# First tile of the next stage taken from pre-scaled copies of x and y, the residual update of that tile done later, five constant matmuls for six

## The chip, the cores and the metric

One Trainium2 chip, one core. The time is that of one launch in device microseconds: the median of three runs for the kernel before, beside the span of one profiled execution. Smaller is better.

## What is computed

Two layers of an encoder step over 320 tokens (256 of a new stream, 64 of a running one), width 1024. The residual x passes three sub-layers per layer, and each is wrapped in two norms:

```python
h = _rms_norm(x, P['ffn1_norm_pre'][l])
x = x + 0.5 * _rms_norm(_swiglu(h, P['ffn1_w_up'][l], P['ffn1_w_down'][l]), P['ffn1_norm_post'][l])
h = _rms_norm(x, P['mix_norm_pre'][l])
m, k_rows, v_rows, s_gla, s_ret = _mixer(h, l, P, past_k, past_v, s_gla0, s_ret0)
x = x + _rms_norm(m, P['mix_norm_post'][l])
h = _rms_norm(x, P['ffn2_norm_pre'][l])
x = x + 0.5 * _rms_norm(_swiglu(h, P['ffn2_w_up'][l], P['ffn2_w_down'][l]), P['ffn2_norm_post'][l])
# _rms_norm(x, g) = x * rsqrt(mean(x * x) + EPS) * g
```

The mixer projects h by W_in, runs a gated linear recurrence, differential attention and retention, and projects by W_out.

## The kernel before, in words

Everything lies transposed: x and y are 8 tiles of 128 features by 320 tokens. Each product is made of three fp32r matmuls (`product`, L629): a weight tile is split into a rounded part w_h (ACT, `hi`) and the rest w_l (DVE, `lo`), and an activation tile into xn_h (ACT, `split_hi`, L1020) and xn_l (DVE, `split_lo`, L1299). Weights come by DMA into six slots.

There are six sub-layers in a row, so five **boundaries** at which a sub-layer's result y is added to x and the next sub-layer starts: in the order of the run, feed-forward 1 to mixer, mixer to feed-forward 2, layer 0 to layer 1, and the first two again in layer 1. At a boundary:

- PE sums the squares of y over the features (`stat_y`, L676 and L680), ACT takes the root (L1025), DVE the reciprocal (L1306), and PE spreads it over the partitions into PSUM, `ps_rs` (`spread`, L688). Then PE runs `keep_busy(6)`: six matmuls of constants whose result nobody reads (L695, two passes each in the trace, so 12 records).
- DVE (`post`) multiplies the y tiles, which already hold the gain of the norm behind the sub-layer, by `ps_rs` (`add_first`, L1310, semaphore y_norm). It adds tile 0 to x itself (L1317); POOL adds tiles 1 to 7 (`add_y`, L519), each when its y tile is multiplied. The semaphore of both is x_new.
- ACT (`pre`) makes xn_h of tile k as soon as x_new says so, and squares x tile k - 1 into y (L1030, semaphore sq_x). DVE makes xn_l of the tile.
- PE's `opening` takes the four first output tiles feature tile by feature tile: step k needs xn_l of tile k and is 12 matmuls. Since the norm in front of the sub-layer is applied to the output, its sum of squares is wanted late: DVE adds squares 0 to 3 (`sum_x`, L1333 to L1337), POOL squares 4 to 7 (L527), and PE takes both in behind step 6 (`stat_x`, L664 and L668). Behind step 7 it spreads the reciprocal (L688 again), for which DVE has first to get through `sum_x`, two `lo` (L511), at the first boundary a few small instructions on the attention's lambda, and L1306.

Every engine works through its own instructions in order; semaphores join them. What stands in `post` and `pre` is therefore the order on DVE and ACT.

Of the kernel before, what the change touches and what calls it, by code (L numbers as in the profile page):

```python
# [9 lines left out]
ACT = mybir.ActivationFunctionType  # L10
ALU = mybir.AluOpType
# [5 lines left out]
T = T_P + T_S  # L17
KD = D // P
KF = D_FF // P
# [22 lines left out]
G_OUT = G_MIX + N_MIX  # L42
G_F2 = G_OUT + N_OUT
GROUPS = G_F2 + KF + KD
# [208 lines left out]
def build(nc, ins, outs, table_at):  # L253
    ctx = ExitStack()
    with ctx:
# [3 lines left out]
        def sem(name):  # L259
            return ctx.enter_context(nc.semaphore(name))  # L260
# [7 lines left out]
        x = sb("x", [P, KD, T])  # L268
        y = sb("y", [P, KD, T])
# [114 lines left out]
        raw_in = [sem(f"raw_in{s}") for s in range(SLOTS)]  # L384
        w_hi, w_lo, w_used = sem("w_hi"), sem("w_lo"), sem("w_used")
        evac = sem("evac")
        x_new = sem("x_new")
        y_norm = sem("y_norm")
        xn_hi, xn_lo = sem("xn_hi"), sem("xn_lo")
        sq_x = sem("sq_x")  # L390
# [113 lines left out]
        def lo(dve, l, u, i=0):  # L504

            if u >= UNITS:
                l, u = l + 1, u - UNITS
            if l < DEPTH:
                s, cols = slot(l, u), blocks_of(u) * P
                dve.wait_ge(w_hi, 6 * i + (l * UNITS + u + 1))  # L510
                dve.tensor_tensor(w_l[s][:, 0:cols], raw[s][:, 0:cols], w_h[s][:, 0:cols], ALU.subtract).then_inc(w_lo, 1)  # L511

        @block.gpsimd
        def _(pool):
            def add_y(l, m):

                for k in range(1, KD):
                    pool.wait_ge(y_norm, (l * 3 + m) * KD + k + 1)
                    pool.tensor_tensor(x[:, k, :], x[:, k, :], y[:, k, :], ALU.add).then_inc(x_new, 1)  # L519

            def sum_x(l, n):
# [104 lines left out]
        def _(pe):  # L626
# [65 lines left out]
            def keep_busy(n):  # L692

                for _ in range(n):
                    pe.matmul(ps_stat[:, 128:384], C("ident"), const[:, 0:256], start=True, stop=True, skip_group_check=True)  # L695

            def ffn(l, u0, g0, norm, n, m):

                def up_pair(i, q, free):
                    pe.wait_ge(w_lo, 6 * i + (l * UNITS + u0 + 2 * q + 2))  # L700
                    if free:
                        pe.wait_ge(evac, 3 * i + (l * GROUPS + g0 + q - 2))
                    for g in range(2):
                        tile_part(slot(l, u0 + 2 * q + g), 2 * q + g, 0, KD)

                opening(l, u0, n, norm, m)
                up_pair(0, 2, False)
                with pe.Fori(1, KF // 3) as i:
                    for q in range(3):
                        up_pair(i, q, True)  # L710
                up_pair(KF // 3, 0, True)
                def down_pair(i):
                    for b in range(2):
                        pe.wait_ge(evac, 2 * i + (l * GROUPS + g0 + KF + b - 1))
                        for t, (a, z_) in enumerate(THIRD):
                            u = u0 + N_UP + 3 * b + t
                            pe.wait_ge(w_lo, 6 * i + (l * UNITS + u + 1))
                            pe.wait_ge(hid_lo, (l * 2 + norm // 4) * KF + z_)
                            for k in range(a, z_):
                                mm = product(ps[:, 2 + b, 0:T], slot(l, u), k - a, hid_h[:, k, :], hid_l[:, k, :], k == 0, k == KF - 1)  # L720
                            mm.then_inc(w_used, 1)
                with pe.Fori(0, KD // 2 - 1) as i:
                    down_pair(i)
                last = l == DEPTH - 1 and norm == 4
                if last:
                    pe.wait_ge(evac, l * GROUPS + g0 + KF)
                    turned(x, X_BANK, 0, KD, x_turn)
                down_pair(KD // 2 - 1)
                stat_y(l, norm + 1, norm // 2)
                if last:  # L730
                    pe.wait_ge(evac, l * GROUPS + g0 + KF + KD - 1)
                    pe.wait_ge(x_turned, 6)
                    turned(y, Y_BANK, 0, KD - 1, y_turn)
                    pe.wait_ge(evac, l * GROUPS + g0 + KF + KD)
                    turned(y, Y_BANK, KD - 1, KD, y_turn)
                else:
                    spread(l, norm + 1)
                    keep_busy(6)

            def turned(t, banks, k0, k1, done):  # L740

# [224 lines left out]
            for l in range(DEPTH):  # L966
                ffn(l, U_F1, G_F1, 0, 0, 0)
                opening(l, U_MIX, 1, 2, 1)
                pe.wait_ge(tables_loaded, PIECES * 16)
                pe.wait_ge(pick_loaded, 16)  # L970
                for kind, *arg in SCHEDULE:
                    if kind == "part":
                        v, k0, k1 = arg
                        if k0 == 0:
                            pe.wait_ge(w_lo, l * UNITS + U_MIX + v + 1)
                            if G_PRIOR[v] is not None:
                                pe.wait_ge(evac, l * GROUPS + G_MIX + G_PRIOR[v] + 1)
                        tile_part(slot(l, U_MIX + v), G_BANK[v], k0, k1)
                    else:
                        mixer_step(l, kind, arg[0] if arg else None)  # L980
                for v in range(OPENING, N_OUT):
                    pe.wait_ge(w_lo, l * UNITS + U_OUT + v + 1)
                    if v >= 6:
                        pe.wait_ge(evac, l * GROUPS + G_OUT + v - 5)
                    tile_part(slot(l, U_OUT + v), v % 6, 0, KD, HEAD_ORDER, xw_h, xw_l)
                stat_y(l, 3, 1)
                spread(l, 3)
                keep_busy(6)
                ffn(l, U_F2, G_F2, 4, 3, 2)


# [3 lines left out]
        def _(act):  # L995
# [20 lines left out]
            def split_hi(l, n, k, src, gain):  # L1016

                scale = 1.0 if gain is None else gains[l][:, gain, k:k + 1]
                dst = xw_h if gain is None else xn_h
                act.activation(dst[:, k, :], src[:, k, :], ACT.Copy, scale=scale).then_inc(xn_hi, 1)  # L1020
# [6 lines left out]
            def pre(l, n, norm, m, u0):  # L1027

                def square(k):
                    act.activation(y[:, k, :], x[:, k, :], ACT.Square).then_inc(sq_x, 1)  # L1030

                for k in range(KD):
                    act.wait_ge(x_new, (l * 3 + m) * KD + k + 1)
                    split_hi(l, n, k, x, norm)
                    if l == 0 and n == 0 and k < 2:
                        hi(act, l, u0 + k + 2)
                    if k:
                        square(k - 1)
                square(KD - 1)
                for v in (4, 5):  # L1040
                    hi(act, l, u0 + v)
                act.preload_act_table(ACT.Sqrt)
                root(l, norm)
# [204 lines left out]
        def _(dve):  # L1248
# [54 lines left out]
            def root(l, n):  # L1303

                dve.wait_ge(ss_sqrt, l * 6 + n + 1)
                dve.reciprocal(inv[:, 0:3], var[:, 0:3]).then_inc(inv_out, 1)  # L1306
                dve.wait_ge(rs_mm, l * 6 + n + 1)

            def add_first(k):
                dve.tensor_tensor(y[:, k, :], y[:, k, :], ps_rs[:, 0:T], ALU.mult).then_inc(y_norm, 1)  # L1310

            def post(l, n, norm, update):

                if update:
                    add_first(0)
                    dve.drain()
                    dve.tensor_tensor(x[:, 0, :], x[:, 0, :], y[:, 0, :], ALU.add).then_inc(x_new, 1)  # L1317
                    add_first(1)
                    add_first(2)
                for k in range(KD):  # L1320
                    if norm is not None:
                        split_lo(l, n, k, x, norm, k)
                    if l == 0 and n == 0 and k == 0:
                        dve.wait_ge(w_lo, 2)
                        lo(dve, l, 2)
                        lo(dve, l, 3)
                    if update and k + 3 < KD:
                        add_first(k + 3)

            def sum_x(l, m):  # L1330

# [30 lines left out]
            def ffn(l, u0, g0, norm):  # L1362
# [50 lines left out]
                if l == DEPTH - 1 and f == 1:  # L1413
                    rows_out(l, norm + 1)
                else:
                    root(l, norm + 1)
                    dve.wait_ge(evac, l * GROUPS + g0 + KF + KD)

# [167 lines left out]
            for l in range(DEPTH):  # L1586
# [34 lines left out]
                for v in range(N_OUT):  # L1621
                    if v < KD - 1:
                        add_square(l, v, 1, v % 2)
                    if v < 5:
                        lo(dve, l, U_OUT + 6 + v)
                    if v == N_OUT - 2:
                        lo(dve, l, U_F2 + 3)
                root(l, 3)
                dve.wait_ge(evac, l * GROUPS + G_OUT + N_OUT)
                begin(l, 3, 4, 2, U_F2, True)  # L1630
# [38 lines left out]
```

## Time and profile before

| | us |
|---|---|
| median of 3 runs | 1392.91 |
| range of these | 1391.44 to 1393.98 |
| profiled execution, its own time | 1392.57 |
| its span, first to last instruction | 1390.8 |
| PE busy / DVE / ACT / POOL | 1352.7 / 804.0 / 634.2 / 132.1 |
| mean granted TensorE clock | 0.989 of 2.4 GHz |

Engines: PE is TensorE's matmul, PEld its weight load, DVE VectorE, ACT ScalarE, POOL GpSimd. A line such as `258.03 0.49 DVE L1317 ...` is the start in us from the span's start, the length, engine, source line, operation and tiles; in brackets stands how long the engine had been idle and what ended that. One engine's entries can overlap by some 0.08 us, since it starts the next instruction while the last one runs out. A line that ends in x2 or more is several instructions taken together.

### The profile page before, as it was taken

What the parts mean: (1) busy time and instruction counts of PE and PEld (TensorE: products, weight loads), DVE (VectorE), ACT (ScalarE), POOL (GpSimd) and SP (SyncE); (2) the same over time, 40 slices, a digit from 0 to 9 for tenths busy, and PEclk for the clock granted to TensorE, in tenths of its full rate; (3) what the DMA queues carried; (4) which work ended last, traced back from release to release, by engine and by line L of the source; (5) the groups of instructions that cost most, each with busy time, mean ns of one, the idle gap of its engine ahead of it and who ended that gap; (6) DMA issues with size and microseconds to landing.
All of it is one profiled execution on the core that took longest, in us unless ns stands there. A gap on an engine that the chain in (4) does not pass through costs nothing.

```text
span 1390.8 us, 24882 instructions
## 1 busy us (share of the span) xinstructions
PE 1352.7 (97%) x9709; PEld 1312.9 (94%) x9709; DVE 804.0 (58%) x1230; ACT 634.2 (46%) x1001; POOL 132.1 (9%) x131
## 2 busy tenths in 40 slices
PE   6999999999989999999999999999899999999998
PEld 6999999988879999999999999999789799999998
DVE  4655543676665665554366555447876477555542
ACT  4544443553455544443355444445435555444333
POOL 2000000361000200000020000003700011000000
PEclk9999999999999999999999999999999899999999
DMA  5655555453234455545545554455333245555552
GB/s 150 191 168 168 164 164 148 127 142 86 80 115 107 107 150 150 151 144 151 152 113 151 148 147 144 144 158 147 87 91 90 89 122 137 151 150 147 144 147 70
DMA packets 351754, 187.51 MB, mean 135 GB/s; under 512 B 6320, under 2 KB 348604, under 8 KB 351688
## 3 DMA queue, kind: packets, MB, share of 16 engines
q1 hardware_dynamic: 348368, 177.49, 45.3%
q0 software_dynamic: 2480, 8.10, 1.7%
q10 hardware_dynamic: 840, 0.99, 0.2%
q8 instruction: 46, 0.75, 0.2%
q14 instruction: 20, 0.16, 0.0%
HBM read 182.24 MB, written 4.33 MB: 134 GB/s over the span
## 4 chain that ended last, share of the span: by engine, by line
PE 90%; DVE 3%; ACT 2%; DMA 2%; issue 1%; DVEq 1%; ACTq 0%; POOL 0%; SPq 0%; POOLq 0%
PE ps L632 28%; PE ps L634 27%; PE ps L633 27%; DMA raw<-in_w_in_dram 1%; PE ps L830 1%; PE ps L931 1%; PE ps L688 1%; PE ps L695 1%; DVE w_l L511 1%; PE ps L805 1%; PE ps L903 1%; ACT w_h L502 1%; PE ps L941 0%; DMA par_in<-in_ret_norm_dram 0%; PE ps L909 0%
## 5 line engine op out<-in xcount | busy, mean ns | idle before, releaser
L632 PE MATMUL ps<-xn_l,w_h 128*128 128x320 f32 x1840 | 579.8, 315 | 2.7 <-DVE xn_l L1299 2.3
L633 PE MATMUL ps<-xn_h,w_l 128*128 128x320 f32 x1840 | 568.9, 309 | 0.0
L634 PE MATMUL ps<-xn_h,w_h 128*128 128x320 f32 x1840 | 568.8, 309 | 0.0
L511 DVE TENSOR_TENSOR w_l<-raw,w_h 128x1024 fp32r<-128x1024 f32 (+1 forms) x340 | 409.0, 1205 | 180.2 <-ACT w_h L502 180.1
L502 ACT ACTIVATE w_h<-raw 128x1024 fp32r<-128x1024 f32 (+1 forms) x342 | 353.4, 1036 | 250.7 <-DMA raw<-in_ffn_w_down_dram 131.8
L632 PEld LDWEIGHTS ps<-xn_l,w_h 128*128 128x128 f32 x1840 | 346.5, 188 | 12.3 <-issue 4.1
L633 PEld LDWEIGHTS ps<-xn_h,w_l 128*128 128x128 f32 x1840 | 346.8, 188 | 0.7
L634 PEld LDWEIGHTS ps<-xn_h,w_h 128*128 128x128 f32 x1840 | 346.5, 188 | 0.0
L632 PE MATMUL ps<-hid_l,w_h 128*128 128x320 f32 x704 | 217.0, 308 | 0.0
L633 PE MATMUL ps<-hid_h,w_l 128*128 128x320 f32 x704 | 216.9, 308 | 0.0
L634 PE MATMUL ps<-hid_h,w_h 128*128 128x320 f32 x704 | 216.9, 308 | 0.0
L632 PEld LDWEIGHTS ps<-hid_l,w_h 128*128 128x128 f32 x704 | 131.9, 187 | 0.0
L633 PEld LDWEIGHTS ps<-hid_h,w_l 128*128 128x128 f32 x704 | 131.9, 187 | 0.0
L634 PEld LDWEIGHTS ps<-hid_h,w_h 128*128 128x128 f32 x704 | 131.9, 187 | 0.0
L1368 DVE TENSOR_TENSOR gate<-ps,rs 128x320 f32<-128x320 f32 x72 | 35.3, 491 | 152.2 <-PE ps L634 152.0
L1065 ACT ACTIVATE gate<-gate 128x320 f32<-128x320 f32 x72 | 34.0, 472 | 138.5 <-DVE gate L1368 138.5
L519 POOL TENSOR_TENSOR x<-x,y 128x320 f32<-128x320 f32 x35 | 37.0, 1088 | 352.7 <-DVE y L1310 352.7
L1069 ACT ACTIVATE hid_h<-up 128x320 f32 (+1 forms) x72 | 34.0, 473 | 67.8 <-DVE up L1374 67.8
L1374 DVE TENSOR_TENSOR up<-up,gate 128x320 f32<-128x320 f32 x72 | 35.4, 492 | 12.0 <-issue 10.9
L1166 ACT ACTIVATE probs<-probs,tiny 128x128 f32<-128x128 f32 (+2 forms) x40 | 19.2, 482 | 49.2 <-DVE tiny L1498 49.2
L1050 ACT ACTIVATE sq<-ps 128x320 f32<-128x320 f32 x48 | 20.8, 432 | 45.9 <-PE ps L634 45.8
L632 PE MATMUL ps<-xw_l,w_h 128*128 128x320 f32 x128 | 41.4, 324 | 0.0
(242 smaller groups left out, 1159.7 us busy)
## 6 DMA issues: line engine op xcount, KB each, us to landing
raw<-in_ffn_w_up_dram SPq DMA_DIRECT2D x176, 512.0 KB, 3.8
raw<-in_ffn_w_down_dram SPq DMA_DIRECT2D x64, 448.0 KB, 3.8
raw<-in_w_in_dram SPq DMA_DIRECT2D x54, 512.0 KB, 3.8
raw<-in_ffn_w_down_dram SPq DMA_DIRECT2D x32, 512.0 KB, 4.1
raw<-in_w_out_dram SPq DMA_DIRECT2D x16, 512.0 KB, 4.1
const<-in_tables_dram POOLq DMA_DIRECT2D x8, 298.0 KB, 4.5
x_in<-in_x_prompt_dram SPq DMA_DIRECT2D x1, 1024.0 KB, 6.6
scores<-in_cache_diff_k_dram POOLq DMA_DIRECT2D x2, 512.0 KB, 5.3
```

Source lines behind the costliest of these rows:

```text
L502: act.activation(w_h[s][:, 0:cols], raw[s][:, 0:cols], ACT.Copy).then_inc(w_hi, 1)
L511: dve.tensor_tensor(w_l[s][:, 0:cols], raw[s][:, 0:cols], w_h[s][:, 0:cols], ALU.subtract).then_inc(w_lo, 1)
L519: pool.tensor_tensor(x[:, k, :], x[:, k, :], y[:, k, :], ALU.add).then_inc(x_new, 1)
L632: pe.matmul(out, w_h[s][:, w], xl, start=first, stop=False)
L633: pe.matmul(out, w_l[s][:, w], xh, start=False, stop=False)
L634: return pe.matmul(out, w_h[s][:, w], xh, start=False, stop=last)
L1050: act.activation(sq[b][:, :], ps[:, bank, 0:T], ACT.Square).then_inc(y_sq, 1)
L1065: act.activation(gate[q][:, :], gate[q][:, :], ACT.Silu).then_inc(silu, 1)
L1069: act.activation(tile(hid_h, v), up[q][:, :], ACT.Copy).then_inc(hid_hi, 1)
L1166: i = act.activation(p, p, ACT.Exp, bias=tiny[:, 8 + 2 * s + m:9 + 2 * s + m], accum_out=tiny[:, 12 + 2 * s + m:13 + 2 * s + m])
L1368: dve.tensor_tensor(gate[q][:, :], ps[:, 2 * q, 0:T], rs[:, :], ALU.mult).then_inc(up_mul, 1)
L1374: dve.tensor_tensor(up[q][:, :], up[q][:, :], gate[q][:, :], ALU.mult).then_inc(prod, 1)
```

## The change

Five places. While PE still sums y's squares, DVE (`prepare_first`) writes two products with the gain of the next norm: x tile 0 into sq[0] and y tile 0 into ssum_x. When `ps_rs` is there, `first_tile` multiplies ssum_x by it and adds it to sq[0]; ACT copies this (no scale any more) into xn_h tile 0, and DVE takes xn_l tile 0 from it. x tile 0 itself is updated behind xn_l tile 2, so ACT squares tiles 0 to 2 only behind xn_h tile 3. `add_first(k + 3)` behind xn_l tile k becomes `add_first(k + 2)`, and POOL's counts on y_norm follow the new order 1, 2, 3, 0, 4 ... 7. `keep_busy` runs five matmuls.

```diff
@@ gpsimd, add_y
                 for k in range(1, KD):
-                    pool.wait_ge(y_norm, (l * 3 + m) * KD + k + 1)
+                    pool.wait_ge(y_norm, (l * 3 + m) * KD + (k if k < 3 else k + 1))
                     pool.tensor_tensor(x[:, k, :], x[:, k, :], y[:, k, :], ALU.add).then_inc(x_new, 1)
@@ tensor, ffn and behind the mixer
-                    keep_busy(6)
+                    keep_busy(5)
@@ scalar, pre
+                update = l * 3 + m
                 for k in range(KD):
-                    act.wait_ge(x_new, (l * 3 + m) * KD + k + 1)
-                    split_hi(l, n, k, x, norm)
+                    if update and k == 0:
+                        act.wait_ge(x_scaled, update)
+                        act.activation(xn_h[:, 0, :], sq[0][:, :], ACT.Copy).then_inc(xn_hi, 1)
+                    else:
+                        act.wait_ge(x_new, KD + (update - 1) * (KD - 1) + k if update else k + 1)
+                        split_hi(l, n, k, x, norm)
...
-                    if k:
+                    if update and k == 3:
+                        act.wait_ge(x_first, update)
+                        square(0)
+                        square(1)
+                        square(2)
+                    elif k and (not update or k > 3):
                         square(k - 1)
@@ vector
+            def prepare_first(l, norm, evicted):
+
+                gain = gains[l][:, norm, 0:1]
+                dve.wait_ge(evac, evicted)
+                dve.drain()
+                dve.tensor_scalar(sq[0][:, :], x[:, 0, :], gain, None, ALU.mult)
+                dve.tensor_scalar(ssum_x[:, :], y[:, 0, :], gain, None, ALU.mult)
+                dve.drain()
+
+            def first_tile(l, n, update):
+
+                dve.tensor_tensor(ssum_x[:, :], ssum_x[:, :], ps_rs[:, 0:T], ALU.mult)
+                dve.drain()
+                dve.tensor_tensor(sq[0][:, :], sq[0][:, :], ssum_x[:, :], ALU.add).then_inc(x_scaled, 1)
+                add_first(1)
+                dve.wait_ge(xn_hi, l * 32 + 8 * n + 1)
+                dve.tensor_tensor(xn_l[:, 0, :], sq[0][:, :], xn_h[:, 0, :], ALU.subtract).then_inc(xn_lo, 1)
+                add_first(2)
+
             def post(l, n, norm, update):
 
                 if update:
-                    add_first(0)
-                    dve.drain()
-                    dve.tensor_tensor(x[:, 0, :], x[:, 0, :], y[:, 0, :], ALU.add).then_inc(x_new, 1)
-                    add_first(1)
-                    add_first(2)
+                    first_tile(l, n, update)
                 for k in range(KD):
-                    if norm is not None:
+                    if k or not update:
                         split_lo(l, n, k, x, norm, k)
...
-                    if update and k + 3 < KD:
-                        add_first(k + 3)
+                    if update and k == 2:
+                        add_first(0)
+                        dve.drain()
+                        dve.tensor_tensor(x[:, 0, :], x[:, 0, :], y[:, 0, :], ALU.add).then_inc(x_first, 1)
+                    if update and 1 <= k + 2 < KD and k:
+                        add_first(k + 2)
@@ vector, before root(l, norm + 1) at the end of ffn, and before root(l, 3)
+                    prepare_first(*((l, 2) if f == 0 else (l + 1, 0)), l * GROUPS + g0 + KF + 1)
...
+                prepare_first(l, 4, l * GROUPS + G_OUT + 1)
```

## Rows read from the trace of the kernel before

**Rows 1.** The page: the span, and the shares of the chain that ended last.

```profile
span 1390.8 us, 24882 instructions
PE 90%; DVE 3%; ACT 2%; DMA 2%; issue 1%; DVEq 1%; ACTq 0%; POOL 0%; SPq 0%; POOLq 0%
```

**Rows 2.** Timeline of DVE at the first boundary (start, us, instruction, idle before).

```profile
256.25 0.18 DVE L1306 RECIPROCAL inv<-var 128x3 f32<-128x3 f32 x1 [1.68 <-ACT var L1025]
257.45 0.49 DVE L1310 TENSOR_TENSOR y<-y,ps 128x320 f32<-128x320 f32 x1 [1.03 <-PE ps L688]
258.03 0.49 DVE L1317 TENSOR_TENSOR x<-x,y 128x320 f32<-128x320 f32 x1
258.44 0.88 DVE L1310 TENSOR_TENSOR y<-y,ps 128x320 f32<-128x320 f32 x2
259.23 0.97 DVE L1299 SCALAR_TENSOR_TENSOR xn_l<-x,par,xn_h 128x320 fp32r<-128x320 f32 x1
...
260.53 0.77 DVE L1299 SCALAR_TENSOR_TENSOR xn_l<-x,par,xn_h 128x320 fp32r<-128x320 f32 x1
...
267.04 0.81 DVE L1299 SCALAR_TENSOR_TENSOR xn_l<-x,par,xn_h 128x320 fp32r<-128x320 f32 x1 [0.28 <-ACT xn_h L1020]
267.77 1.17 DVE L1333 SCALAR_TENSOR_TENSOR ssum<-y 128x320 f32<-128x320 f32 x1
...
270.10 0.49 DVE L1337 TENSOR_TENSOR ssum<-ssum,y 128x320 f32<-128x320 f32 x1
270.51 2.35 DVE L511 TENSOR_TENSOR w_l<-raw,w_h 128x1024 fp32r<-128x1024 f32 x2
...
274.32 0.18 DVE L1306 RECIPROCAL inv<-var 128x3 f32<-128x3 f32 x1
```

**Rows 3.** Timeline of ACT at the same boundary.

```profile
258.56 0.56 ACT L1020 ACTIVATE xn_h<-x,par 128x320 fp32r<-128x320 f32 x1 [0.82 <-DVE x L1317]
259.90 0.56 ACT L1020 ACTIVATE xn_h<-x,par 128x320 fp32r<-128x320 f32 x1 [0.78 <-POOL x L519]
260.36 0.46 ACT L1030 ACTIVATE y<-x 128x320 f32<-128x320 f32 x1
```

**Rows 4.** Timeline of POOL there: its first addition alone, all seven, the last two sums.

```profile
259.00 0.86 POOL L519 TENSOR_TENSOR x<-x,y 128x320 f32<-128x320 f32 x1 [1.06 <-DVE y L1310]
259.00 7.40 POOL L519 TENSOR_TENSOR x<-x,y 128x320 f32<-128x320 f32 x7 [1.06 <-DVE y L1310]
...
267.64 2.04 POOL L527 TENSOR_TENSOR ssum_x<-ssum_x,y 128x320 f32<-128x320 f32 x2
```

**Rows 5.** Timeline of PE there: constants, first product, sum of x's squares, spread.

```profile
257.25 2.76 PE L695 MATMUL ps<-const 128*128 128x256 f32 x12
260.26 0.41 PE L632 MATMUL ps<-xn_l,w_h 128*128 128x320 f32 x1 [0.26 <-DVE xn_l L1299]
...
272.68 0.72 PE L664 MATMUL ps<-const,ssum 128*128 128x1 f32 x6
...
275.78 0.83 PE L688 MATMUL ps<-const,inv 128*128 128x128 f32 x6
```

**Rows 6.** The group of ACT's copies without a scale (min/median/max ns).

```profile
L1020 ACT ACTIVATE xw_h<-y x16: 470/473/476, 415.5 to 1117.6; 128x320 fp32r<-128x320 f32 x16
```

**Rows 7.** Timeline of PE at the second and the third boundary.

```profile
457.93 3.79 PE L695 MATMUL ps<-const 128*128 128x256 f32 x12
461.37 0.50 PE L632 MATMUL ps<-xn_l,w_h 128*128 128x320 f32 x1
...
698.85 4.44 PE L695 MATMUL ps<-const 128*128 128x256 f32 x12
702.94 0.50 PE L632 MATMUL ps<-xn_l,w_h 128*128 128x320 f32 x1
```

**Rows 8.** Busy time by stretch: window, length, PE, PEld, DVE, ACT, POOL, granted clock, DMA.

```profile
457.00:458.00 1.00, 1.00 (x7) 1.00 (x6) 0.00 (x0) 0.00 (x0) 0.00 (x0) 0.50 0.21 63
...
700.00:701.00 1.00, 1.00 (x4) 0.80 (x3) 1.00 (x4) 0.56 (x1) 0.41 (x1) 0.50 0.00 0
940.00:943.00 3.00, 3.00 (x17) 2.38 (x15) 2.42 (x5) 0.63 (x2) 1.92 (x4) 1.00 1.01 340
```

**Rows 9.** Timeline of DVE at the second boundary: the reciprocal, and the tiles' start.

```profile
456.30 0.17 DVE L1306 RECIPROCAL inv<-var 128x3 f32<-128x3 f32 x1 [1.48 <-ACT var L1025]
458.17 0.49 DVE L1310 TENSOR_TENSOR y<-y,ps 128x320 f32<-128x320 f32 x1 [1.70 <-PE ps L688]
...
459.96 0.97 DVE L1299 SCALAR_TENSOR_TENSOR xn_l<-x,par,xn_h 128x320 fp32r<-128x320 f32 x1
```

More of the change, by code:

```diff
@@ L386, in build @@
         evac = sem("evac")
-        x_new = sem("x_new")
+        x_new, x_first = sem("x_new"), sem("x_first_tile")
+        x_scaled = sem("first_tile_times_next_gain")
         y_norm = sem("y_norm")
@@ L987, in _ @@
                 spread(l, 3)
-                keep_busy(6)
+                keep_busy(5)
                 ffn(l, U_F2, G_F2, 4, 3, 2)
```

## The prediction

> **What bounds the kernel now.** I read the page first: PE carries 90% of the chain that ended last [rows 1], so an edit on DVE, ACT or POOL counts only where PE waits for it. It can do that at the five boundaries, so I went through the timelines of all engines there. At the first one, take DVE's first multiply behind the spread, 257.45, as zero; all times below count from it. The multiply runs to 0.49, the update of x tile 0 from 0.58 to 1.07, two more multiplies to 1.87, and xn_l of tile 0 from 1.78 to 2.75 [rows 2]. ACT's part lies between, 1.11 to 1.67 [rows 3]. The constants end at 2.56, the first product starts at 2.81, released by xn_l [rows 5]. So this chain binds by 0.25 us. Then PE doesn't wait: seven steps bring it to the sum of x's squares at 15.23, and its spread stands at 18.33 [rows 5]. DVE has its sum of squares ready at 13.14 (270.10 + 0.49) and POOL at 12.23 [rows 2, 4]: 2.1 us to spare.
>
> The two boundaries around the mixer in layer 1, the fourth and fifth, repeat this within 0.03 us. The second and third differ: the granted clock is 0.50 there, the lower level of 1.2 GHz, while it is 1.00 at the fourth [rows 8]. The constants then take 3.79 and 4.44 us instead of 2.76 [rows 5, 7], and it is they that end last: at the second, xn_l is ready at 460.93 [rows 9], the first product starts at 461.37 [rows 7].
>
> **A collision that sets the prices.** POOL's first addition takes 0.86 us; seven take 7.40, so 1.09 each once DVE works beside it [rows 4]. DVE's xn_l of tile 0 takes 0.97 beside that first addition, which ends at 2.41, 0.34 before xn_l does; L1333 takes 1.17 beside POOL's sums, L1337 only 0.49 after them [rows 2, 4]. Every DVE instruction with both inputs in SBUF behaves so, and the multiplies by PSUM do not (0.49 and 0.44 each). I read it as taking turns: whoever comes second waits for the other to finish. DVE then needs 0.34 more (0.49 alone), POOL 0.75 (0.86 alone). With handovers of 0.04 us from DVE to ACT (258.52 to 258.56) and from POOL to ACT (259.86 to 259.90), and 0.08 from DVE to POOL (the first of the two multiplies ends at 258.92, POOL starts at 259.00) [rows 2 to 4], stepping through the old order with these prices gives 13.12 for DVE's sums and 12.20 for POOL's, against 13.14 and 12.23 in the trace. I use the same prices for the new order.
>
> The Trainium skill's page "SBUF — State Buffer", section "Who interferes with whom", says the same as a rule: a DVE instruction with two SBUF inputs and a GpSimd one that reads SBUF exclude each other, and order of issue decides who waits. By that rule the change's first tile can't be early, since its subtraction has two SBUF inputs; the trace agrees with the rule (0.97 against 0.49).
>
> **prepare_first.** Two instructions of at most 0.49 us and two drains of about 0.09, some 1.1 us. DVE sat idle for 1.68 us before this reciprocal at the first boundary and 1.48 at the second [rows 2, 9]; the other three lie at about 1.6. Hidden, cost 0. If the cover went, each 0.1 us would be 0.1 us of PE's wait for the spread. No row shows a DVE instruction of this kind beside the four DMAs that POOL issues there; from both sides, 0 to +0.3 us at two boundaries; I take 0, because the preparation is nearly through when they start.
>
> **The first tile.** Multiply to 0.49, addition to 1.07, as before. ACT's copy has no scale and takes 0.47 for 0.56 [rows 3, 6]: 1.11 to 1.58. One multiply less stands ahead of xn_l, so DVE is ready at 1.62 instead of 1.87. But POOL starts on tile 1 at 1.55 as before and holds its turn to 2.41. So xn_l ends at 2.75 as before, and the first product starts at 2.81 as before. Gain 0; if DVE came first, it would end at 2.11, a gain of up to 0.65. The margin is 0.07 us; I take 0, by the row of 0.97.
>
> **Five constants.** Two passes less, 2.76 / 12 x 2 = 0.46 us. At three boundaries xn_l binds, and PE only idles 0.7 us instead of 0.25: gain 0. At the second the constants would end at 460.91, xn_l at 460.93: gain 0.38. At the third they still bind: gain about 0.44.
>
> **The later tiles.** This is where I see the cost. y tile 2 is multiplied behind xn_l tile 0 (2.66 to 3.13, before: 1.39 to 1.87), so POOL, which used to have work waiting, starts tile 2 at 3.21 and xn_l tile 1, at 3.06, now goes ahead of it: tile 2 on POOL ends at 4.30 for 3.48. xn_h of tile 2 follows to 4.90, xn_l to 5.43. POOL's tile 3 waits for a count of 4 on y_norm, which is the multiply of tile 0, placed behind xn_l tile 2: it ends at 5.83. POOL adds tile 3 from 5.91 to 6.77 (before: 3.46 to 4.57), and the late update of x tile 0 waits for its turn to 7.11. xn_h of tile 3 to 7.37, xn_l to 7.92. Queued behind on ACT are three squares, 7.28 to 8.48, so xn_h of tile 4 starts at 8.71. From there each y multiply is one tile less ahead than before, and the rest goes at DVE-to-POOL-to-ACT round-trip pace: xn_l ends at 9.77, 10.65, 12.49, 13.58 for tiles 4 to 7.
>
> Does PE wait in its steps? Step k starts at 3.05 + 1.76 k (15.37 less 3.05 over seven steps): 8.33 for tile 3 (ready 7.92), 10.09 for tile 4 (9.77), 13.61 for tile 6 (12.49). No, by 0.3 us at the closest. But tile 7 is ready at 13.58 instead of 10.40 (267.04 + 0.81 [rows 2]), and DVE's three sums come behind it: 2.8 us as before, so 16.34. PE wants them at 15.37, the start of its first of six (the row's 15.23 holds 0.14 of overlap), and starts at 16.39: a new wait of 1.0 us. POOL's sums, at 15.4, are not last.
>
> **Behind that.** DVE's two `lo` move to 18.6 (15.41 + 3.2), the reciprocal to 18.8; PE wants its spread at 18.47 + 1.0 = 19.5, so this is covered at four boundaries. At the first, small instructions stand between, and the reciprocal starts at 16.87, 1.46 behind the `lo` [rows 2]: it ends at 20.2, PE starts at 20.3 instead of 19.5: +0.8 us more, once.
>
> **The sum.** First boundary 1.0 + 0.8; fourth and fifth 1.0 each. At the second PE starts its steps at 3.20 and wants the sums 0.5 later than at the first: the floor of 16.39 costs 0.5 in all. At the third it starts at 3.89, the floor lies 0.2 below the old time: -0.2. Together 1.8 + 0.5 - 0.2 + 2.0 = **+4.1 us**. The profiled execution took 1392.57 us (span 1390.8), 0.34 below the median of the runs, so its boundaries stand for the median's; 1392.9 + 4.1 = **1397.0 us**.
>
> **Bounds.** If the turns fall better (POOL and DVE never meet at tiles 3 and 5), the sums come 0.7 us sooner: +0.3 per boundary, 0.5 for the first's spread, minus 0.8 for the constants, so about +1. If two more turns go against DVE, 0.45 each, the sums come 0.9 later: +4.5 in all, 1401.5.
>
> **Rivals.**
> (a) *Hidden.* The sums come by 15.4 after all, and only the constants count: -0.8 us, 1392.1. For it: 2.1 us of slack before. Against it: tile 0's detour alone puts POOL's tile 3 back by 2.4 us against the seven close additions before [rows 4]. 15%.
> (b) *As the edit is built.* DVE's subtraction goes ahead of POOL's tile 1, PE starts 0.65 sooner at three boundaries, and the sums are in time: 3 x 0.65 + 0.8 = 2.8, so 1390.1 us. It decides at 0.07 us of order, and needs (a) too. 6%. (That the first tile is not earlier, the change not doing what it says, is part of my forecast.)
> (c) *The clock.* With the pause of PE before the first step grown from 0.25 to 0.7 us and 1 us of waiting at the sums, the lower level comes at more boundaries. It costs 5.1 - 4.0 = 1.1 us at one (reciprocal to first product, 461.37 - 456.30 against 260.26 - 256.25 [rows 2, 5, 7, 9]), and three boundaries are still free of it: 1397.0 + 3.3 = 1400.3. It bites from the second extra boundary on. For it: the pauses are longer. Against it: the pause before the constants (2.6 us), which the clock fell behind, is unchanged. 13%.
> The forecast keeps 66%.
>
> **Numbers.** A measurement of this kernel tells about 0.2% (2.8 us) from no change: above 1395.7 is slower, below 1390.1 faster. The forecast spreads from 1394 to 1399.5 and is slower in nine of ten cases, 0.59; with (c), 0.72. Same: the rest of the forecast and (a), 0.22. Faster: 0.06. The range 1392.8 to 1401.3 takes in the bounds and part of (a).
>
> **What would show it.** In the changed kernel's profile: PE idle before L664 (about 1 us at three boundaries, released by DVE's ssum, L1337's place), which has none now; the first product still 2.8 us behind DVE's first multiply, and the subtraction at 0.7 us or more; a gap in POOL's additions between tiles 2 and 3 of about 1.6 us; a wait before the spread at the first boundary only; the reciprocal of y at its old distance from ACT's root. I am wrong if L664 shows no wait, if POOL's additions run on closely, or if the subtraction of tile 0 takes 0.49.

## The result and the profile after

The changed kernel takes 1404.05 us (median of 6 runs, 1402.72 to 1407.83); the kernel before, in the same session, 1392.19 (1391.21 to 1393.98). The ratio is 1.0086, interval 1.0075 to 1.0096: **11.9 us slower**. The forecast was 1397.0, in a range that ended at 1401.3. The sign and the place were right; the forecast loss of 4.1 us was a third of what came.

The page of the changed kernel, its span and the shares of the chain that ended last (lines of [rows 1]):

```profile
span 1401.9 us, 24897 instructions
...
PE 86%; DVE 6%; ACT 3%; DMA 2%; POOL 1%; DVEq 1%; issue 1%; SPq 0%; ACTq 0%; POOLq 0%
```

PE fell from 90% to 86% of the chain, DVE rose from 3% to 6%, and ACT and POOL have a part. The waits of PE say where (engine and line, for whom, us in total, times, longest):

```profile
PE ps L665 <- DVE ssum L1367: 4.4, 5, 1.1
PE ps L689 <- DVE inv L1317: 4.2, 6, 1.3
```

The first line is new. Before, PE never waited for the sum of x's squares; now it does at all five boundaries. L1367 is the old L1337, L665 the old L664.

The timeline of DVE at the fourth boundary of the changed kernel, which answers to [rows 2] (the first multiply behind the spread is at 944.88):

```profile
944.88 0.49 DVE L1334 TENSOR_TENSOR ssum_x<-ssum_x,ps 128x320 f32<-128x320 f32 x1 [1.03 <-PE ps L689]
945.45 0.49 DVE L1336 TENSOR_TENSOR sq<-sq,ssum_x 128x320 f32<-128x320 f32 x1
945.86 0.48 DVE L1321 TENSOR_TENSOR y<-y,ps 128x320 f32<-128x320 f32 x1
946.48 1.16 DVE L1339 TENSOR_TENSOR xn_l<-sq,xn_h 128x320 fp32r<-128x320 f32 x1
...
950.90 1.21 DVE L1356 TENSOR_TENSOR x<-x,y 128x320 f32<-128x320 f32 x1
...
957.97 0.80 DVE L1310 SCALAR_TENSOR_TENSOR xn_l<-x,par,xn_h 128x320 fp32r<-128x320 f32 x1 [0.29 <-ACT xn_h L1021]
958.69 1.17 DVE L1363 SCALAR_TENSOR_TENSOR ssum<-y 128x320 f32<-128x320 f32 x1
...
961.03 0.49 DVE L1367 TENSOR_TENSOR ssum<-ssum,y 128x320 f32<-128x320 f32 x1
```

And POOL there, which answers to [rows 4]:

```profile
946.43 0.85 POOL L520 TENSOR_TENSOR x<-x,y 128x320 f32<-128x320 f32 x1 [0.98 <-DVE y L1321]
948.11 1.12 POOL L520 TENSOR_TENSOR x<-x,y 128x320 f32<-128x320 f32 x1 [0.83 <-DVE y L1321]
950.89 0.88 POOL L520 TENSOR_TENSOR x<-x,y 128x320 f32<-128x320 f32 x1 [1.66 <-DVE y L1321]
952.59 1.96 POOL L520 TENSOR_TENSOR x<-x,y 128x320 f32<-128x320 f32 x2 [0.82 <-DVE y L1321]
```

The subtraction for xn_l of tile 0 (946.48) starts 0.05 us after POOL's first addition (946.43), takes 1.16 us and ends at 947.64, 2.76 behind the first multiply, where the kernel before had 2.75. The shorter first tile brought nothing. POOL, which made its seven additions without a pause, now stops 0.83, 1.66 and 0.82 us for y. The longest stop is ahead of tile 3. "The change" gives the order of the multiplies as 1, 2, 3, 0, so the one of tile 3 is the third; but the condition `k < 3` in the diff lets POOL wait for a count of 4, that is for the multiply of tile 0 as well. DVE's sums end at 961.52, 16.64 behind the first multiply, for 13.14 before.

What PE makes of this (timeline of PE, same boundary; [rows 5] before):

```profile
947.68 0.41 PE L633 MATMUL ps<-xn_l,w_h 128*128 128x320 f32 x1 [0.68 <-DVE xn_l L1339]
...
961.58 0.83 PE L665 MATMUL ps<-const,ssum 128*128 128x1 f32 x6 [1.08 <-DVE ssum L1367]
...
965.53 0.47 PE L633 MATMUL ps<-xn_l,w_h 128*128 128x320 f32 x1
...
966.33 0.83 PE L689 MATMUL ps<-const,inv 128*128 128x128 f32 x6
```

13.90 us pass from the first product to the sums, for 12.43. Then 4.75 to the spread, for 3.10: a matmul of step 7 takes 0.47 us in its row instead of 0.31. The busy times of that stretch (columns as in [rows 8]) give the granted clock as 0.50, the lower level of 1.2 GHz:

```profile
963.00:966.00 3.00, 3.00 (x12) 3.00 (x13) 0.88 (x2) 0.17 (x1) 0.00 (x0) 0.50 0.17 26
```

Before it fell, PE had stood still for 1.08 us and then run the twelve one-column records of the sums. The five boundaries side by side, in us, read from the starts of L1306, of the first product, of L664 and of L688 in the profile of each kernel:

| boundary | 1 | 2 | 3 | 4 | 5 | sum |
|---|---|---|---|---|---|---|
| reciprocal to first product, before | 4.01 | 5.07 | 5.10 | 4.02 | 4.02 | 22.2 |
| after | 4.66 | 4.70 | 4.37 | 4.00 | 4.00 | 21.7 |
| first product to sums, before | 12.42 | 12.51 | 12.51 | 12.43 | 12.43 | 62.3 |
| after | 13.25 | 13.91 | 13.51 | 13.90 | 13.90 | 68.5 |
| sums to spread, before | 3.10 | 3.10 | 3.10 | 3.10 | 3.09 | 15.5 |
| after | 3.55 | 4.27 | 3.21 | 4.75 | 4.43 | 20.2 |

So of 11.1 us of span, 6.2 lie between the first product and the sums, 4.7 behind the sums, and -0.5 ahead of the first product. The rest, 0.7, lies elsewhere. (The medians differ by 11.9 us, 0.8 more than these two profiled spans.) Of the 4.7 us, 0.45 at the first boundary are a wait for the reciprocal (0.18 us of idle time for DVE's inv stand in PE's row there); the other 4.3 go with the lower level of the clock.

The granted clock by stretch shows where that level stood. Before, it was 0.50 at the constants of the second and third boundary and 1.00 at those of the others. In the changed kernel it is 0.50 at the constants of the first, second and third, and 0.50 behind the sums at the second, fourth and fifth. The pauses of PE at the sums were 0.58, 1.09, 0.55, 1.08 and 1.08 us.

### The profile page after: what moved, and what is told of

Its sections match the earlier page's. It is cut to its first block, busy times and chain, and to the rows that moved or that the text cites. A ratio compares the mean times of both kernels' runs of the same rounds, so it can differ in the third digit from the quotient of the medians.

```text
span 1401.9 us, 24897 instructions
## 1 busy us (share of the span) xinstructions
PE 1359.8 (97%) x9699; PEld 1318.2 (94%) x9699; DVE 810.4 (58%) x1250; ACT 632.9 (45%) x1001; POOL 127.6 (9%) x131
## 4 chain that ended last, share of the span: by engine, by line
PE 86%; DVE 6%; ACT 3%; DMA 2%; POOL 1%; DVEq 1%; issue 1%; SPq 0%; ACTq 0%; POOLq 0%
PE ps L633 26%; PE ps L634 26%; PE ps L635 26%; POOL x L520 1%; DMA raw<-in_ffn_w_up_dram 1%; ACT xn_h L1021 1%; DVE xn_l L1310 1%; PE ps L689 1%; PE ps L831 1%; PE ps L932 1%; PE ps L806 1%; DMA raw<-in_w_in_dram 1%; DVE w_l L512 1%; PE ps L942 0%; PE ps L904 0%
## 5 line engine op out<-in xcount | busy, mean ns | idle before, releaser
L520 POOL TENSOR_TENSOR x<-x,y 128x320 f32<-128x320 f32 x35 | 33.9, 978 | 372.3 <-DVE y L1321 372.3
L1404 DVE TENSOR_TENSOR up<-up,gate 128x320 f32<-128x320 f32 x72 | 35.4, 492 | 11.2 <-issue 10.1
```

What stands on the lines that cost most here:

```text
L1404: dve.tensor_tensor(up[q][:, :], up[q][:, :], gate[q][:, :], ALU.mult).then_inc(prod, 1)
```

## The experiments

Theory S: the sum of x's squares comes too late because DVE and POOL get through the tiles later; PE waits, and the granted clock falls behind the wait. Rivals: C, the clock fell because a constant matmul is missing; P, the preparation or the new first tile costs the time; L, the shorter lead of the y multiplies alone.

**POOL's addition of tile 3 released by the right count (after_count3).**

```diff
-                    pool.wait_ge(y_norm, (l * 3 + m) * KD + (k if k < 3 else k + 1))
+                    pool.wait_ge(y_norm, (l * 3 + m) * KD + (k if k < 4 else k + 1))
```

> The changed kernel, with POOL's addition of tile 3 waiting for a count of 3 on y_norm (the multiply of tile 3) and not 4 (that of tile 0, behind xn_l tile 2). Theory S (the sum of x's squares comes late, PE waits for it, and the granted clock falls behind that wait): stepping through the order with the trace's prices, DVE's sums end at 15.9 behind its first multiply for 16.6, so PE's wait before L665 shrinks from 1.1 to about 0.4 us, the start of the sums moves 0.7 us forward at each of five boundaries, and some of the falls of the clock behind it go: 1404.0 - 3.5 - 2 = 1398 us. Theory C (the missing sixth constant matmul lets the clock fall): no change, 1404. Theory P (the preparation or the new first tile costs it): no change, 1404.

1399.3 us, ratio to before 1.0047 (1.0030 to 1.0064). The first product to the sums is 13.16 to 13.19 everywhere, for 13.25 to 13.91. PE's row at the fourth boundary:

```profile
959.34 0.83 PE L665 MATMUL ps<-const,ssum 128*128 128x1 f32 x6 [0.58 <-DVE ssum L1367]
```

One digit takes some 40% of the loss away, as S has it, though the wait is 0.6 us and not 0.4. The sums to the spread still take 3.5 to 4.2, and the granted clock is 0.50 behind the sums at all five boundaries of this profile, where the changed kernel had three. So the forecast that some falls would go did not come true, and a pause of 0.6 us was enough here; at the first and third boundary of the changed kernel, where the clock had been low at the constants, pauses as long brought none.

**Six constants again (after_six).**

```diff
-                    keep_busy(5)
+                    keep_busy(6)
```

> The changed kernel with six constant matmuls again. Theory S: PE waits for the sums, not for the start, so nothing moves at the boundaries where xn_l tile 0 binds, and the sums end when they did: 1404 within 1.5 us. Theory C: the falls of the clock that the change added go, 5 of them at 1 to 1.7 us each: 1397 us, with the mean granted clock back at 0.989.

1403.7 us, 1.0078 (1.0061 to 1.0095). No time came back, and the mean granted clock was 0.982 to 0.985 as in the changed kernel. C falls as the cause of the loss. But "nothing moves" was not right either: in this profile the clock was 0.50 at the constants of the first, second and fourth boundary, the first products came 2.9 us later in all than in the changed kernel, and the stretch from there to the sums was 2.5 us shorter in all. The sums set the time, whenever PE starts.

**The lead of three tiles restored, with POOL's counts to match, everything else of the change kept (after_lead3).**

```diff
-                    pool.wait_ge(y_norm, (l * 3 + m) * KD + (k if k < 3 else k + 1))
+                    pool.wait_ge(y_norm, (l * 3 + m) * KD + (k if k < 5 else k + 1))
...
                 add_first(1)
+                add_first(2)
                 dve.wait_ge(xn_hi, l * 32 + 8 * n + 1)
                 dve.tensor_tensor(xn_l[:, 0, :], sq[0][:, :], xn_h[:, 0, :], ALU.subtract).then_inc(xn_lo, 1)
-                add_first(2)
+                add_first(3)
...
-                    if update and 1 <= k + 2 < KD and k:
-                        add_first(k + 2)
+                    if update and k and k + 3 < KD:
+                        add_first(k + 3)
```

> The changed kernel, with DVE's multiplies of y again three tiles ahead (2 before xn_l tile 0, 3 behind it and so on) and POOL's counts to match. Pre-scaled first tile, late update of x tile 0, late squares, the preparation and five constants all stay. Theory S: stepping through with the trace's prices, DVE's sums end at 14.6 behind its first multiply, 0.7 us before PE wants them: no wait, clock as in the kernel before, and 0.4 us less at boundaries where the constants end last: 1392 to 1393.5 us. Theory P (preparation and first tile cost it): 1402 to 1404.

1392.4 us, 0.9996 (0.9987 to 1.0006). The whole loss is gone, with the preparation, the pre-scaled tile, the late update, the late squares and five constants still in. P falls. The new counts also take away POOL's needless wait for tile 0, so this run undoes two things together, the shorter lead and that count; after_count3 undid the count alone. DVE and PE at the fourth boundary (two timelines of this kernel):

```profile
953.91 0.49 DVE L1368 TENSOR_TENSOR ssum<-ssum,y 128x320 f32<-128x320 f32 x1
```

```profile
955.05 0.72 PE L665 MATMUL ps<-const,ssum 128*128 128x1 f32 x6
...
958.15 0.83 PE L689 MATMUL ps<-const,inv 128*128 128x128 f32 x6
```

The sums are ready 0.65 us before PE starts on them, no wait stands in PE's row, and the spread follows 3.10 later.

**Only the shorter lead, in the kernel before (before_lead2).**

```diff
                     add_first(1)
-                    add_first(2)
...
-                    if update and k + 3 < KD:
-                        add_first(k + 3)
+                    if update and k + 2 < KD:
+                        add_first(k + 2)
```

> The kernel before, with only DVE's multiplies of y one tile less ahead (tile 2 behind xn_l tile 0, tile k + 2 behind tile k). Stepping through gives DVE's sums at 14.9 for 13.1: inside the 2.1 us of slack, so no wait of PE and 1393 us within 1.5. If the shorter lead alone is the cause (rival L: it starves POOL, and the first tile's detour is innocent), PE waits at L664 and the time is 1399 us or more.

1392.5 us, 0.9997 (0.9988 to 1.0007). L falls too. The last sum ends 0.26 us before PE wants it (956.94 + 0.49 against 957.69). Behind the first multiply DVE's sums end at 13.1 in the kernel before, at 15.0 with the shorter lead alone and at 14.6 with the detour for tile 0 alone (after_lead3). Either fits into the 2.1 us of slack. Together they reach 15.9 (POOL's count put right) and 16.6 (the changed kernel), and PE wants them at 15.2.

**The late sum alone, in the kernel before**, with six copies (before_late_sum) and with eight (before_late_sum8):

```diff
                 post(l, n, norm, update)
+                if update:
+                    for _ in range(6):
+                        dve.tensor_copy(rs[:, :], ps_rs[:, 0:T])
+                        dve.drain()
                 sum_x(l, m)
```

> The kernel before, with six copies of the spread into rs (overwritten later) and a drain behind each, 6 x 0.58 = 3.5 us, ahead of DVE's sum of squares at the five boundaries. Nothing else of the change is in it: first tile, order, six constants as before. Theory S: the sums end at 16.6 behind the first multiply for 13.1, as in the changed kernel, PE waits 1.1 us at the sums and the clock falls behind it: 1392.2 + 11 = 1403 us (and at least 1392.2 + 5 x 1.4 = 1399 if the clock doesn't follow). Theories C and P: the late sum costs only its wait, 0 to 3 us, 1392 to 1395, since they put the 12 us elsewhere.

1393.1 us, 0.9997 (0.9988 to 1.0007). This missed: the copies delayed the end of the sums, counted from the first multiply, only by 2.2 to 2.5 us, since the sums no longer ran beside POOL and took 0.49 us each. At the fourth boundary they ended at 957.23 and PE started at 957.29 with no wait. As a dose it is useful: late by nearly all of the slack costs nothing.

> As before_late_sum, with eight copies for six. Six moved the end of DVE's sums only from 14.3 to 16.5 to 17.3 us behind the reciprocal (the copies also took away collisions with POOL), just under the point from which PE waits; the changed kernel has 17.8. Two more copies, 1.16 us, bring it to 17.7 to 18.0. Theory S: now PE waits 0.9 to 1.2 us at L664 at each boundary, the start of the sums moves by 1.2 to 1.5 us, and with what the clock does behind it the kernel takes 1393 + 7 to 11 = 1400 to 1404 us. If the 12 us have another source (the first tile, the order): 1393 to 1396.

1403.1 us, 1.0068 (1.0045 to 1.0091). Two copies more, and ten microseconds come. DVE and PE at the fourth boundary:

```profile
958.29 4.43 DVE L1350 COPY rs<-ps 128x320 f32<-128x320 f32 x8
962.80 0.49 DVE L1333 SCALAR_TENSOR_TENSOR ssum<-y 128x320 f32<-128x320 f32 x1
```

```profile
964.49 0.83 PE L664 MATMUL ps<-const,ssum 128*128 128x1 f32 x6 [1.10 <-DVE ssum L1337]
```

PE's waits for the sums add up to 4.6 us (4.4 in the changed kernel), the first product to the sums to 67.8 (68.5), the sums to the spread to 20.6 (20.2), and the mean granted clock of the runs lies between 0.982 and 0.988. The copies hold up everything that DVE does behind them, but PE's rows show waits for the sums at all five boundaries and for the reciprocal only at the first, 0.17 us. So a late sum by itself makes a loss of the changed kernel's size (1.0068 and 1.0086, intervals that overlap); this is shown, not argued.

**Constants in the place of the wait.** Both in the changed kernel (after_fill) and in the kernel before (before_fill):

```diff
                     if i == KD - 2:
+                        if l or n:
+                            keep_busy(3)
                         stat_x(l, norm, m)
```

> The changed kernel, with three constant matmuls (2 passes each, 1.4 us) put into PE's queue ahead of the sum of x's squares at the five boundaries, so that PE works while it would wait. If the clock falls because of PE's wait (second half of theory S), it no longer falls behind the sums, which is worth 1.2 to 1.6 us at three boundaries, while the constants are hidden in 1.1 us of wait and cost up to 0.3 us each: 1404.0 - 4 + 1 = 1401 us, with the spread starting 3.1 to 3.5 us behind L665 everywhere (now 4.3, 4.8 and 4.4 at the second, fourth and fifth). If the wait has nothing to do with the clock: 1404 to 1405.5, with as many stretches at a granted 0.5 as before.

after_fill: 1402.75 us, 1.0076 (1.0059 to 1.0093). The row of this kernel at the fourth boundary, which answers to `963.00:966.00` above:

```profile
962.00:965.00 3.00, 3.00 (x25) 3.00 (x25) 2.08 (x3) 0.22 (x2) 0.00 (x0) 1.00 0.01 3
```

The granted clock is 1.00, as it is behind the sums at the other four. The sums to the spread went back to 3.10 to 3.17 at all five boundaries, and the mean granted clock of the runs, between 0.982 and 0.985 in the changed kernel, lies between 0.986 and 0.989 here, the level of the kernel before (between 0.986 and 0.992). So the falls behind the sums came from the pause. But 4.5 us behind the sums were bought with 1.4 ahead of them and 1.2 ahead of the first product, and the total moved by 1.3, within the intervals. What the falls cost in all is not shown by this.

> The kernel before, with three constant matmuls ahead of the sum of x's squares at the five boundaries: PE reaches the sums 1.4 us late, but busy, at full clock. It prices the delay without a pause. If a delay of 1.4 us costs 1.4 us wherever it comes from, 1393.0 + 5 x 1.4 = 1400 us and the spread 3.1 us behind the sums everywhere; what the changed kernel (1404.0) and before_late_sum8 (1403.1) take beyond this is then the clock that falls behind a pause. If it takes 1403 or more, the clock has no part in it and a delay costs more than itself.

before_fill: 1402.6 us, 1.0066 (1.0053 to 1.0078). First product to sums 13.71 to 13.81, sums to spread 3.10, no wait at the sums, clock 0.987 to 0.990. This missed too: five delays of 1.3 us cost 9.2 us (by the ratio, as in the next three runs; 10.0 by the medians). In its profile 1.2 us of the excess are one landing of W_in behind the fourth boundary (PE waits 2.13 us for gv_tok there, 0.89 before), and two stretches of low clock lie elsewhere. Of its 10.1 us more of span only 5.4 lie at the boundaries. The rest lies in the two mixer stretches, from the spread of boundary 1 to the reciprocal of boundary 2 (182.95 us for 180.52) and from 4 to 5 (184.20 for 181.25); the feed-forward stretches between boundaries agree within 0.1 us. But the first of these also takes 182.98 us in the profile of before_lead2 and 182.94 in that of before_dve1 (below), whose medians are those of the kernel before. One profile of each kernel can't tell whether the delay brings this rest. Three more runs asked how the remainder goes.

> One constant matmul (0.46 us) ahead of the sum of x's squares at five boundaries of the kernel before, for three in before_fill. If a delay costs itself: 1392.8 + 2.3 = 1395.1 us. If it costs 1.5 times itself, as three constants did (9.5 us for 6.4): 1396.2. If there is a fixed cost of some 3 us as soon as PE comes late at all: 1398.

One constant (before_fill1): 1396.4 us, 1.0027 (1.0017 to 1.0037): +3.8 (2.4 to 5.2) for 5 x 0.45.

> Six constants (2.7 us) at the same place. If a delay costs itself: 1392.8 + 5 x 2.7 = 1406.3 us. At 1.5 times: 1413. With a fixed cost of 3 us: 1409.3.

Six constants (before_fill6): 1407.2 us, 1.0107 (1.0093 to 1.0122): +14.9 (13.0 to 17.0) for 5 x 2.6 = 13.

> Nine constants for six behind the spread of y's root: the same 1.4 us as in before_fill, but ahead of the first product, which waits 0.25 us for xn_l anyway, and not ahead of the sums. Each boundary is delayed by 1.1 to 1.4 us. If the remainder belongs to the place (what waits behind the sums), 1392.8 + 6.2 = 1399 us. If any delay of PE costs 1.5 times itself, 1402.

Nine constants (before_nine): 1398.4 us, 1.0040 (1.0026 to 1.0053): +5.6 (3.6 to 7.4). The first product came 0.7 us later where the clock was full and 1.3 where it was low, which is 3 x 0.7 + 2 x 1.3 = 4.7 us with the clock as in the kernel before.

In these four runs a delay costs itself plus 1 to 3 us that don't grow in step with it. Neither "1.5 times" (it forecast 1413 for six) nor a fixed 3 us (1398 for one lies outside) is right for all; where that rest lies is **left open**.

**A better opening.** DVE adds tile 1 (before_dve1), or tiles 1 and 2 (before_dve2), to x itself, with five constants (here tile 1; for two tiles, POOL starts at 3, and the block stands for `k < 2` with `x[:, k + 1, :]` and `add_first(k + 2)`):

```diff
-                for k in range(1, KD):
+                for k in range(2, KD):
...
                     add_first(1)
-                    add_first(2)
                 for k in range(KD):
                     if norm is not None:
                         split_lo(l, n, k, x, norm, k)
+                    if update and k == 0:
+                        dve.drain()
+                        dve.tensor_tensor(x[:, 1, :], x[:, 1, :], y[:, 1, :], ALU.add).then_inc(x_new, 1)
+                        add_first(2)
...
-                    keep_busy(6)
+                    keep_busy(5)
```

> The kernel before, with DVE adding y tile 1 to x itself, between xn_l tile 0 and the multiply of tile 2, and five constants. POOL has nothing to do when xn_l tile 0 is made, so that should take 0.55 us for 0.97 and the first product start 0.45 to 0.5 us earlier at the boundaries where xn_l binds. xn_l tile 1 then meets POOL's tile 2 and ends at 4.6 behind the first multiply, 0.2 us after PE wants it. Net 0.2 to 0.4 us less at each of five boundaries: 1393.2 - 1.5 = 1391.7 us, and the sums still in time (13.9). If the taking of turns is not what delays xn_l tile 0, it starts where it did: 1393 us, xn_l at 0.97.

1393.1 us, 0.9999 (0.9990 to 1.0009). DVE at the fourth boundary:

```profile
942.60 0.55 DVE L1299 SCALAR_TENSOR_TENSOR xn_l<-x,par,xn_h 128x320 fp32r<-128x320 f32 x1 [0.23 <-ACT xn_h L1020]
943.24 0.49 DVE L1324 TENSOR_TENSOR x<-x,y 128x320 f32<-128x320 f32 x1
943.65 0.88 DVE L1310 TENSOR_TENSOR y<-y,ps 128x320 f32<-128x320 f32 x2
944.44 0.99 DVE L1299 SCALAR_TENSOR_TENSOR xn_l<-x,par,xn_h 128x320 fp32r<-128x320 f32 x1
```

With POOL idle xn_l of tile 0 takes 0.55 us, for 0.97, and the first product comes 3.50 behind the reciprocal, for 4.02. Tile 1 then meets POOL, takes 0.99, and PE gives the half microsecond back in step 1 (12.96 to the sums for 12.43).

> As before_dve1, with DVE adding y tile 2 to x as well, behind xn_l tile 1, and POOL starting with tile 3. before_dve1 moved the first product 0.5 us forward (3.50 us behind the reciprocal for 4.02) and lost it in step 1 (12.96 us from the first product to the sums for 12.43), since xn_l tile 1 met POOL's tile 2 and took 0.99 us. Now POOL is idle then: xn_l tile 1 should take 0.55, tile 2 meet POOL's tile 3 and end 6.1 us behind DVE's first multiply, just when PE wants it. So 0.4 to 0.5 us less at each of five boundaries: 1393.0 - 2.2 = 1390.8 us. If another tile's wait takes the place, 1393.

1393.3 us, 1.0005 (0.9995 to 1.0014). The same with tile 2, timelines of DVE and PE:

```profile
946.43 0.99 DVE L1299 SCALAR_TENSOR_TENSOR xn_l<-x,par,xn_h 128x320 fp32r<-128x320 f32 x1
```

```profile
947.48 0.41 PE L632 MATMUL ps<-xn_l,w_h 128*128 128x320 f32 x1 [0.27 <-DVE xn_l L1299]
```

The wait only moved to step 2. No version beat the kernel before.

## Why the prediction was wrong

- **What binds, and the taking of turns: right.** The same prices that gave the old order gave the new one: at the fourth boundary each of the seven tile ends that the prediction names came within 0.31 us. xn_l of tile 0 ends at 2.76 (forecast 2.75), POOL's gap ahead of tile 3 is 1.66 us (1.6), the sums end at 16.64 (16.34), the first boundary's reciprocal is the only one to hold up the spread, which stands 20.26 behind the first multiply (20.3), and that boundary takes 1.9 us more (1.8). before_dve1 shows the turns directly, 0.55 against 0.97. The rule of the Trainium skill's page "SBUF — State Buffer" (section "Who interferes with whom") holds in these rows.
- **First tile and preparation: right, nothing.** DVE had 0.78 to 0.96 us left before the reciprocal at the five boundaries; after_lead3 prices both at zero. Rival (b) fell: DVE came 0.05 to 0.13 us behind POOL at the five boundaries, and the subtraction took 1.07 to 1.16 us.
- **The wait at the sums: right step, mis-sized.** Where the clock is full, the forecast put the sums 1.0 us later behind the first product; they come 1.47 later. 0.3 come from DVE, whose sums end that much later (xn_l alone takes 0.55 us, I took 0.49). 0.15 is the overlap of the first sum with the last product, which goes when PE has stood still and which I had set aside. (PE also lost 0.2 us in steps 3 and 4, where I saw no wait; the sums came later still, so that cost nothing.) At the second and third boundary I let the low clock absorb most (0.9 and 0.2 us from the first product on); it measured 1.40 and 1.00. From the first product to the sums that makes 6.2 us for 4.1. With what was won ahead of the first product, it is 5.7 for 3.3 of the whole forecast of 4.1.
- **The failed step: the clock.** The forecast's sum has no term for a fall of the clock at the sums. It stood only in rival (c), with 13%, a price of 1.1 us taken from a stretch filled with constants, and the argument that the pause ahead of the constants is unchanged. It is unchanged (at the second boundary 1.28 us of idle time in both profiles; the 2.6 us count the one-column matmuls of y's sums as well). The pause ahead of the sums is what was new. Where the clock falls behind it, it falls on twelve real products, and the sums to the spread take 1.2 to 1.7 us more at three boundaries. Forecast behind the sums: 0.8 us for the first reciprocal and nothing for the clock. Measured: 0.45 and 4.3. Over the runs the mean granted clock lies between 0.986 and 0.992 in the kernel before, between 0.982 and 0.985 in the changed one. A straight line through 69 runs of the kernel before gives 0.8 us for each 0.001, so a fall of some 0.005 goes with about 4 us; this is a correlation, and an estimate.
- **Bounds.** I bounded the collisions (sums 0.9 us later) and the clock (three boundaries at 1.1), but one at a time. Both terms came out larger, and the range ended 2.8 us short.
- **What stays open** is the exact split: before_fill pays 9.2 us for delays of 6.4 with no pause at the sums. That the falls take 4.3 us where they stand is read from one profile; that the kernel would be about 4 us faster without them is an estimate, not shown.

## What to carry to other kernels

Before moving work down a queue, find who reads its last result and how much time that one has: here 2.1 us between DVE's sums and PE, which two edits of 1.5 to 1.8 us could each use but not both. Step through the queues with prices from the trace, collisions included; here it gave the end of each tile to 0.3 us. Check each semaphore count against the new order; one digit was worth some 40% of the loss. And when PE gets a new pause, give the sum a term for the products behind it at the lower clock, and not only one for the pause.

## What the runs showed of the hardware

- A DVE instruction of 128x320 with two inputs in SBUF takes 0.49 to 0.55 us with POOL idle, 0.97 to 1.21 when it starts just behind a POOL addition of 0.85 to 0.88; coming 0.05 us later, in one row 0.01, was enough.
- Five pauses of 0.3 to 1.5 us at the sums brought 0.003 (before_late_sum8) and 0.005 (after) less of mean granted clock over the runs, though PE was busy for over 12 us ahead of each. With three constants in the pause, the clock behind the sums stayed at 1.00.
- One kernel's runs spread with the granted clock: twelve of before_fill1 lie between 1392.3 us at a mean of 0.992 and 1401.3 at 0.985.
